# Routing stage of a two-block transformer kernel: expert gather ahead of the bias product, and a mask moved from GpSimd to VectorE

## What is computed

```python
logits = (xt @ router_w + router_b)
top_v, top_e = lax.top_k(logits, TOP_K)            # 4 of 32 experts
gate = jax.nn.softmax(top_v, axis=-1)
# for each expert e, over the tokens routed to it
hb = xb @ w1[e] + b1[e]
g, u = hb[:, :D_EXPERT], hb[:, D_EXPERT:]
g = jnp.minimum(g, SWIGLU_LIMIT); u = jnp.clip(u, -SWIGLU_LIMIT, SWIGLU_LIMIT)
y = ((u + 1.0) * (g * jax.nn.sigmoid(g * SWIGLU_ALPHA))) @ w2[e] + b2[e]
out = jnp.zeros((N, D)).at[row_tok].add(y * row_w[:, None])
# later, in the neighbourhood attention of the second block
s_win = jnp.einsum('brqhd,brkwhd->bhrqkw', qg, k_blk) * scale + bias
s_win = jnp.where(col_ok[:, None, :], s_win, NEG_INF)
```

## Time and profile before

| | |
|---|---|
| median of 3 runs | 2906.81 us (2906.61 to 2908.82) |
| profiled execution | 2904.19 us, span 2902.0 us |
| TensorE busy | 2758.6 us, 95% of the span |
| VectorE busy | 2113.6 us, 73% |
| ScalarE busy | 1534.3 us, 53% |
| GpSimd busy | 11.0 us, 7 instructions |
| mean granted TensorE clock | 0.97 of full speed |
| transfers | 776.07 MB, 267 GB/s over the span |

### The profile page before, as it was taken

The page is one execution under the profiler, slowest core; times in us unless marked ns, Lnnn a source line. Parts: engine busy times, 40 slices in busy tenths (PEclk is TensorE's granted clock), DMA queues, the critical chain, the costliest instruction groups (busy, mean ns, idle before and its releaser), DMA issues.

```text
span 2902.0 us, 43416 instructions
## 1 busy us (share of the span) xinstructions
PE 2758.6 (95%) x17494; PEld 2471.4 (85%) x17494; DVE 2113.6 (73%) x1872; ACT 1534.3 (53%) x1294; POOL 11.0 (0%) x7
## 2 busy tenths in 40 slices
PE   5999998999999999999998899999999999999998
PEld 4888886778777777777786899999979999999998
DVE  5435547999999999999998968777446766754453
ACT  0023226888888888888885334334444434332342
POOL 0000000000000000000000100000000000000000
PEclk8999997999999999999999899999999999999999
DMA  9753336999999999999997677677516767755452
GB/s 376 249 180 125 132 132 246 378 375 375 364 373 364 376 377 378 380 379 380 376 376 274 189 262 271 247 257 247 204 38 217 276 248 245 274 179 175 146 189 72
DMA packets 172400, 776.07 MB, mean 267 GB/s; under 512 B 12112, under 2 KB 37712, under 8 KB 121328
## 3 DMA queue, kind: packets, MB, share of 16 engines
q1 hardware_dynamic: 168352, 767.08, 70.2%
q10 hardware_dynamic: 3920, 7.11, 0.8%
HBM read 773.10 MB, written 1.05 MB: 267 GB/s over the span
## 4 chain that ended last, share of the span: by engine, by line
PE 62%; DVE 21%; issue 13%; ACT 3%; DVEq 1%; DMA 0%; ACTq 0%; SPq 0%
PE psum L1195 36%; DVE w_low L2259 11%; PE psum L1149 7%; PE psum L1570 4%; PE psum L1335 4%; ACT w_high L917 2%; PE psum L1607 2%; PE psum L1274 2%; DVE mod_sums L1844 1%; PE psum L1543 1%; DVE arena L2278 1%; PE psum L1293 1%; PE psum L1383 1%; DVE arena L2291 1%; DVE hid L2293 1%
## 5 line engine op out<-in xcount | busy, mean ns | idle before, releaser
L2259 DVE TENSOR_TENSOR w_low<-ring,w_high 128x2048 fp32r<-128x2048 f32 x396 | 882.1, 2287 | 40.2 <-ACT w_high L917 36.2
L917 ACT ACTIVATE w_high<-ring 128x2048 fp32r<-128x2048 f32 x396 | 736.9, 1906 | 90.3 <-PE psum L1570 88.4
L2395 DVE TENSOR_TENSOR w_low<-ring,w_high 128x2048 fp32r<-128x2048 f32 (+1 forms) x199 | 432.7, 2184 | 325.8 <-ACT w_high L1011 322.6
L1011 ACT ACTIVATE w_high<-ring 128x2048 fp32r<-128x2048 f32 (+1 forms) x199 | 362.3, 1829 | 576.9 <-PE psum L1195 501.2
L1195 PE MATMUL psum<-h_high,w_high 128*128 128x256 f32 x2080 | 592.6, 285 | 28.9 <-ACT h_high L1024 21.0
L1195 PE MATMUL psum<-h_high,w_low 128*128 128x256 f32 x2080 | 594.8, 286 | 0.0
L1195 PE MATMUL psum<-h_low,w_high 128*128 128x256 f32 x2080 | 592.1, 286 | 0.0
L1195 PEld LDWEIGHTS psum<-h_high,w_high 128*128 128x128 f32 x2080 | 403.9, 194 | 31.2 <-issue 22.9
L1195 PEld LDWEIGHTS psum<-h_low,w_high 128*128 128x128 f32 x2080 | 398.7, 193 | 0.0
L1195 PEld LDWEIGHTS psum<-h_high,w_low 128*128 128x128 f32 x2080 | 397.9, 191 | 0.0
L1570 PE MATMUL psum<-w_high,xg 128*128 128x512 f32 x1056 | 347.4, 410 | 16.5 <-DVE w_low L2259 11.4
(11 more groups left out here) (278 smaller groups left out, 3289.2 us busy)
## 6 DMA issues: line engine op xcount, KB each, us to landing
ring<-in_exp_w SPq DMA_DIRECT2D x396, 1024.0 KB, 7.7
ring<-in_ffn_w SPq DMA_DIRECT2D x135, 1024.0 KB, 5.3
ring<-in_mod_w SPq DMA_DIRECT2D x96, 1024.0 KB, 5.5
ring<-in_ffn_w SPq DMA_DIRECT2D x40, 768.0 KB, 4.7
ring<-in_w_in SPq DMA_DIRECT2D x24, 1024.0 KB, 8.9
ring<-in_even_w_in SPq DMA_DIRECT2D x12, 1024.0 KB, 7.0
ring<-in_conv_w_in SPq DMA_DIRECT2D x12, 1024.0 KB, 5.0
ring<-in_w_branch SPq DMA_DIRECT2D x6, 1024.0 KB, 5.0
```

The lines of the kernel that those rows point to most:

```text
L917: act.activation(high_ap(j, D), slot_ap(PLAN.moe_slot + j), ACT.Copy).then_inc(sem("expert_high_ready" + c.x), 1)
L1011: act.activation(high_ap(m, cols), slot_ap(s, 2, cols), ACT.Copy).then_inc(sem("w_high_ready"), 1)
L2259: dve.tensor_tensor(low_ap(PLAN.moe_slot + j, D), slot_ap(PLAN.moe_slot + j), high_ap(j, D).bitcast(F32), ALU.subtract).then_inc(sem("expe ...
L2395: dve.tensor_tensor(low_ap(s, cols), slot_ap(s, 2, cols), high_ap(m, cols).bitcast(F32), ALU.subtract).then_inc(sem("w_split"), 1)
```

## The change

The additional turn's result now begins with the bias product, so `acc` starts from zero. The bias product's operands move: `gateT` to the end of the arena, `b2_rows` to a buffer of `mod_sums`. The gather follows the gate turn directly (with one pad where three were). ScalarE splits part 0 before the exponentials of the routing and parts 1 to 3 before the copies of the gather. The 16 one-column memsets of the top-k become 8, placed before the mixer's last addition, and one copy. The squared gains move from before the additional turn into `add_over`. The position mask moves from GpSimd to VectorE, in front of the first scores.

```diff
@@ plan
-    p.unit("bias_sum", 2)
@@ ScalarE, routing
+            high(first_turn(0), 0)
             route = small[:, 0:448]
             for b in range(TB):
                 act.wait_ge(sem("top_ready"), b + 1)
...
             act.activation(gateT[0:N_EXPERTS, :], unit(u)[0:N_EXPERTS, 0:T], ACT.Copy).then_inc(psum_free[u % 4], 1)
+            high(first_turn(0), 1, 2, 3)
...
-            high(first_turn(0), 0, 1, 2, 3)
+            for half in range(2):
+                await_unit(act, U["gather"] + half)
+                gathered(half, unit(U["gather"] + half), "")
             most = many(act)
@@ TensorE, routing
             mm.then_inc(psum_full, 1)
-            await_freed(pe, u)
-            pe.wait_ge(sem("b2_landed"), 16)
-            for k in range(DC):
-                u = U["bias_sum"] + k // 4
-                if k % 4 == 0:
-                    open_unit(pe, u)
-                mm = pe.matmul(unit(u)[:, (k % 4) * T:(k % 4 + 1) * T], b2_rows[0:E, k * P:(k + 1) * P], gateT[0:E, :],
-                               start=True, stop=True)
@@ TensorE, additional turn
+                def biases():
+                    await_freed(pe, U["gate_turn"])
+                    pe.wait_ge(sem("b2_landed"), 16)
+                    for k in range(DC):
+                        name = "result" + "b" * (k // 4)
+                        if k % 4 == 0:
+                            c.open_unit(pe, name)
+                        pe.matmul(c.unit(name)[:, (k % 4) * T:(k % 4 + 1) * T], b2_rows[0:N_EXPERTS, k * P:(k + 1) * P],
+                                  gateT[0:N_EXPERTS, :], start=(k % 2 == 0), stop=False, skip_group_check=True)
...
                 if over:
                     turn_rows("up0_turn", "up0", "up_rows")
+                    biases()
                     down(0, range(DC), 8)
@@ VectorE
+            dve.memset(acc, 0.0)
+            for n in range(4):
+                for b in range(TB):
+                    at = 36 * b + N_EXPERTS + n
+                    last = dve.memset(small[:, at:at + 1], -(n + 1.0) * 1e37)
+            link(last)
             mods_of("w_out")
...
-            for n in range(4):
-                for b in range(TB):
-                    link(dve.memset(vals[:, 36 * b + E + n:36 * b + E + n + 1], -(n + 1.0) * 1e37))
-                    link(dve.memset(top[:, 8 * b + 4 + n:8 * b + 5 + n], -(n + 1.0) * 1e37))
+            link(dve.tensor_copy(top.rearrange("p (b e) -> p b e", b=TB)[:, :, 4:8],
+                                 vals.rearrange("p (b e) -> p b e", b=TB)[:, :, E:E + 4]))
...
-            for half in range(2):
-                u = U["bias_sum"] + half
-                await_unit(dve, u)
-                free(dve.tensor_copy(acc[:, 4 * half:4 * half + 4, :], chunks(u)), u)
-                await_freed(dve, u)
...
                 def add_over():
                     acc_to_x(steps.link)
+                    squared_gains()
@@ the mask: GpSimd before, VectorE after, in front of na_soft(0)
-            pool.wait_ge(sem("rpb_landed"), 16 * ROWS)
-            pool.tensor_tensor(view, view, mask, ALU.add).then_inc(sem("rpb_masked"), 1)
-            dve.wait_ge(sem("rpb_masked"), 1)
+            dve.wait_ge(sem("rpb_landed"), 16 * ROWS)
+            link(dve.tensor_tensor(view, view, mask, ALU.add))
```

More of the change, by code:

```diff
@@ L342 @@
 MOD_BUFFERS, MOD_BUFFER_BEFORE = mod_buffers()
+assert MOD_BUFFERS[L1_MODS][0] not in MOD_BUFFERS[L1_MODS - 1]
 GAIN2_BUFFER = [b for b in range(MOD_SUMS) if b not in MOD_BUFFERS[L1_MODS]][0]
@@ L890, in _, with high @@
                 act.activation(h_nat_high[:, n, :], unit(u)[:, :], ACT.Copy).then_inc(sem("h_nat_high_ready"), 1)
+            for q in PLAN.high_before:
+                await_release(act, q)
+            def high(c, *slots):
+                for j in slots:
+                    c.await_used(act, j - HIGHS)
+                    c.await_slot(act, j)
+                    act.activation(high_ap(j, D), slot_ap(PLAN.moe_slot + j), ACT.Copy).then_inc(
+                        sem("expert_high_ready" + c.x), 1)
+            high(first_turn(0), 0)
             route = small[:, 0:448]
@@ L1604, in result @@
                         name = "result" + "b" * (k // 4)
-                        if k % 4 == 0 and e == 0:
+                        if k % 4 == 0 and e == 0 and not over:
                             c.open_unit(pe, name)
@@ L1608, in result @@
                                        moe_buf(f"y_rows{e}")[:, k * P:(k + 1) * P], moe_buf(f"selT{e}"),
-                                       start=(e == 0 and k % 2 == 0), stop=final, skip_group_check=True)
+                                       start=(e == 0 and k % 2 == 0 and not over), stop=final,
+                                       skip_group_check=True)
                         if k % 4 == 3 and final:
                             mm.then_inc(c.full, 1)
+                def biases():
[7 more added lines that the diff above has]
+                                  gateT[0:N_EXPERTS, :], start=(k % 2 == 0), stop=False, skip_group_check=True)
                 def gather_next(half):
@@ L2268, in acc_to_x, with squared_gains @@
                 done(last)
+            def squared_gains():
+                for k in range(DC):
+                    gain = vec("final1")[:, k:k + 1]
+                    last = dve.tensor_scalar(mod_sums[:, GAIN2_BUFFER, k * P:(k + 1) * P], ones, gain, gain, ALU.mult, ALU.mult)
+                link(last)
+                link(dve.tensor_scalar(mod_sums[:, GAIN2_BUFFER, :], mod_sums[:, GAIN2_BUFFER, :], 1.0 / D, None, ALU.mult))
             def experts(c, steps, last=False, over=False):
@@ L2345, in _ @@
                 steps.leave(PAIRS)
-            for k in range(DC):
-                gain = vec("final1")[:, k:k + 1]
-                last = dve.tensor_scalar(mod_sums[:, GAIN2_BUFFER, k * P:(k + 1) * P], ones, gain, gain, ALU.mult, ALU.mult)
-            link(last)
-            link(dve.tensor_scalar(mod_sums[:, GAIN2_BUFFER, :], mod_sums[:, GAIN2_BUFFER, :], 1.0 / D, None, ALU.mult))
             experts(over_turn(busiest_expert(dve)), steps, over=True)
```

20 lines of the change are left out of this document (4 added, 16 removed).

## The result

| | before | after |
|---|---|---|
| median of 4 runs each, same chip | 2906.85 us (2906.61 to 2908.82) | 2886.26 us (2881.71 to 2889.26) |
| profiled execution | 2904.19 us, span 2902.0 | 2887.47 us, span 2885.7 |
| TensorE busy | 2758.6 us | 2766.9 us |
| mean granted clock | 0.970 | 0.969 |

The ratio is 0.9927, with a 95% interval of 0.9913 to 0.9941: faster, by 20.6 us or 0.7%. I had said 2875 us and a range up to 2885, so the time lies 1.3 us outside. Later comparisons ran the same kernel twice more, at 2877.7 and 2879.9 us; the median of all its 12 runs is 2880.1.

The account below looks back on a forecast made before the run. VectorE and TensorE were taken as nearly full in the unchanged expert loop, so gains lay in waits around it: 16.7 + 4.8 + 9.4 = 30.9 us off, median 2875.9, stated as 2875 us, range 2868 to 2885.

Parts of the forecast that it names:

- Place one: Routing to the first expert product: TensorE starts the loop at 450.2 instead of 466.93 us, gain 16.7 (14.5 to 18.5).
- Rival (b): Routing: ScalarE or the loop entry takes part of the gather's gain; place one gives 14 or less, 2879 us; chance 0.12.
- Place two: Additional turn and the stage behind it: down projection starts 2.5 us earlier and runs at full clock, another 2.3; gain 4.8.
- the pause: Additional turn: TensorE's gap ahead, 4.82 us before, becomes some 1.5 us with the bias product, so the clock should hold.
- rival (a): Additional turn: the clock stays at half, so place two gives 1 us and the time is 2880 us; chance 0.13.
- Place three: Mask off GpSimd: VectorE's 10.17 us instruction and TensorE's 6.55 us wait go; gain 9.4 us (6.5 to 9.8).
- The loop: Expert loop, 16 turns: unchanged, 1081.5 us from first expert product to loop's end; wrong if off by over 5.
- Rival (d): Expert loop settles into a worse phase in each of 16 turns; at 2.5 us a turn 2916 us; chance 0.02.

Follow-up runs that it names:

- 128 rows and the pause: Changed kernel with the bias product over all 128 rows instead of 32, the wait ahead of it kept: 2875.74 us, ratio 0.9892.
- both edits: Changed kernel with the bias product over 128 rows and two PSUM banks of the additional turn's result exchanged, so it need not wait: 2872.15 us, ratio 0.9882.
- the mask alone: Kernel before with only the position mask moved from GpSimd to VectorE: 2897.04 us, ratio 0.9962.
- the wide product between the projections: Changed kernel with the bias product over 128 rows, placed between the additional turn's gate and up projections: 2879.19 us, ratio 0.9906.
- the narrow one: Changed kernel with the 32-row bias product placed between the additional turn's gate and up projections: 2879.63 us, ratio 0.9912.

## Why the prediction missed, point by point

**Place one** was forecast at 16.7 us and gave 16.4 to 16.5 in the three profiles, against the first profile of before. Its steps hold too: from the mixer's last addition the mask of the top four was expected at 24.4 us and came at 24.4, the gather at 28.8 and came at 28.9, the end of the second copy at 37.0 and came at 37.1; the loop's entry took 1.64 us where I had 1.4. Rival (b) did not come.

**Place two is the step that failed.** It said that the bias product runs at full clock, that the down projection starts 2.5 us sooner, and that a full clock in it gives another 2.3: 4.8 us together. The entry was right: 2.5 to 3.8 us less in B. But the product took 6.72, 5.97 and 6.00 us where 3.69 was forecast, the down projection's first pair took 1.22 us and not 0.7, and C grew by 2.6 to 3.1, so B and C together gave between -0.2 and 0.7 us, which is rival (a), held at 0.13. The prediction had the row that speaks for it, the half clock through 16 us of 32-row product and gather, read it rightly as a sign that small products may not hold the clock, and still gave the length of the pause the larger weight. With 128 rows and the pause, as the prediction had it, B and C give 1085.09 - 1082.49 = 2.6 and 33.03 - 32.36 = 0.7 us: 3.3. With both edits they give 1085.09 - 1082.98 = 2.1 and 33.03 - 30.60 = 2.4: 4.5 us. So the 4.8 came nearly in full only with 128 rows and without the pause that the prediction had left in.

The Trainium skill, "TensorE: Matmul & The Clock Gate", Part 1: The HAM clock gate, says that sustained matmul activity lifts the clock and idling lowers it. The trace agrees for the wide product between the projections (1.00 in every slice) and for the waits of 3.3 to 4.9 us (half clock behind each). It does not agree for the narrow one, where TensorE was busy for 2.00 us of each 2 us slice and the clock fell to 0.51, nor for the gather, where it was busy for 7.00 us of 7.00 at 0.50.

**Place three** was forecast at 9.4 us (6.5 to 9.8). D gave 10.3 in the first pair of profiles, and 9.6 between the mean of the two profiles before and that of the three after. The two profiles of before differ by 3.0 us in D, and those of after by 3.5, so that its size is known to some 3 us. The cause is shown by the mask alone. The Trainium skill, "GPSIMD Engine Reference", section 1 (Specifications), says that GpSimd shares its memory interfaces with VectorE and that they contend when a VectorE instruction has two inputs there; the trace agrees: such an instruction took 10.17 us instead of 1.28.

**The loop** repeats: from the first expert product to the end of the loop's last additions it was 1081.7 us after, against 1081.3 (the prediction's 1081.5 ends at the squared gains, 0.2 us later). Rival (d) did not come.

**The range** was too narrow on its slow side for a second reason. It took "some spread of the runs" as 2 to 3 us. The first comparison lost 10.2 us of its profiled gain (16.3 where the places sum to 26.5) in stretches where the work is the same, and the kernel before itself ran between 2898.2 and 2915.5 us in the later comparisons. The missing 4.8 us of place two alone would have given 2880, inside the range; the clock of the other stages put it outside. That 2886 came in the first comparison and 2878 and 2880, inside the range, in the later ones is the luck of the run, and place two failed in all of them.

## What to carry to other kernels

A product with few rows that has to stand in the middle of full work is worth trying with all 128 rows, with zeros for the missing ones: here it took the same time (3.61 us against 3.72), and what followed kept the full clock. It is no rule for every product, as the gather shows with 128 rows at half clock. Where something is moved into another engine's wait, ask which clock TensorE will have there, and count a row of half clock for a busy TensorE as evidence against "it is busy, so it will be fast". And a chain of stages is compared by distances between marks, since the clock of stages that are not full moved the whole by 10 us here from run to run.

## What the runs showed of the hardware

The clock fell to half while TensorE was busy without a gap in and behind 32-row products (1.00 to 0.51), and did not fall with 128 rows in the same place; a 128-row product begun at half clock was followed by work at full clock (its records took from 0.634 down to 0.379 us, 5.38 in all). Through the gather, 32 records of 128 rows by 128 columns without a gap, it stayed at 0.50 for 7.00 us.

GpSimd's addition over 128 x 4096 elements (10.69 and 9.84 us) held up the first VectorE instruction that started behind it until 1.1 us past its own end, in both profiles of before: 10.17 and 10.20 us instead of 1.28, for an instruction with two inputs in SBUF. The VectorE instruction that was already running kept its usual length: a subtraction with two inputs in the first profile (2.28 us, 1.7 of them beside GpSimd), and in the second a sum of the very kind that was then held up (1.28 us, 0.8 beside GpSimd). So the order of starting tells the two apart, and not the kind; whether VectorE instructions with one input are held up was not tried. On VectorE the same addition took 4.42 us.

Twice, work that came later by 2.7 or 2.8 us was back to within 0.6 and 1.3 us behind the additional turn, for the most part because the half-clock stretch fell on other instructions (the bias product took 4.75 and 5.47 us instead of 5.97 to 6.72). A gain in front of such a stretch is not passed on one to one.
